# Delta rule in a small model's mixer: two units in step, value blocks inside the first inverse, an earlier gate slab, head norms by tokens, decay products on one engine

## What is computed

```python
def wkv7_scan(r, w, k, v, kk, a):
    def step(state, inp):
        r_t, w_t, k_t, v_t, kk_t, a_t = inp
        sk = jnp.einsum('bhvk,bhk->bhv', state, kk_t)
        state = (state * w_t[:, :, None, :]
                 - sk[..., None] * (a_t * kk_t)[:, :, None, :]
                 + v_t[..., None] * k_t[:, :, None, :])
        return state, jnp.einsum('bhvk,bhk->bhv', state, r_t)

# in rwkv7_time_mix (8 heads of 64):
    kk = heads(k * k_k)
    kk = kk / jnp.maximum(jnp.sqrt(jnp.sum(kk * kk, axis=-1, keepdims=True)), 1e-12)
    y = wkv7_scan(r_h, w_h, k_h, v_h, kk, a_h)
    mean = jnp.mean(y, axis=-1, keepdims=True)
    var = jnp.mean(jnp.square(y - mean), axis=-1, keepdims=True)
    y = (y - mean) * lax.rsqrt(var + EPS_GN)
    y = y * lnx_g + lnx_b
    y = (y + bonus) * g
```

## Time and profile before

| | us |
|---|---|
| median of 3 runs | 3098.65 (3093.9 to 3120.61) |
| profiled execution | 3099.2 |
| its span | 3097.6 |
| PE busy | 2847.0 (92%) |
| DVE busy | 1756.4 (57%) |
| ACT busy | 997.8 (32%) |
| POOL busy | 194.6 (6%) |

### The profile page before, as it was taken

One profiled execution on the slowest core, in us unless ns is written; L12 is line 12 of the kernel. 1 busy time (PEld: TensorE's weight loads), 2 busy tenths in 40 slices (PEclk: granted clock), 3 DMA queues, 4 the chain that ended last, 5 costly groups with the idle time before them and its releaser, 6 DMA issues.

```text
span 3097.6 us, 44761 instructions
## 1 busy us (share of the span) xinstructions
PE 2847.0 (92%) x18701; PEld 2328.5 (75%) x18701; DVE 1756.4 (57%) x2310; ACT 997.8 (32%) x1335; POOL 194.6 (6%) x244
## 2 busy tenths in 40 slices
PE   6979999988999999988889989999978899899997
PEld 6768888777678888767768768887657768688886
DVE  6667777768558777575364443334583473443334
ACT  5543222233442222242333332223432332332222
POOL 3100000000000000010040000000010040000000
PEclk9989999979999999899999999999888999999999
DMA  4214655412025555221003322222220012223221
GB/s 155 82 56 139 183 166 166 139 46 78 1 86 176 170 166 166 69 66 45 3 15 100 109 82 95 95 95 77 68 76 3 3 48 89 95 89 100 97 92 58
DMA packets 239083, 282.12 MB, mean 91 GB/s; under 512 B 7492, under 2 KB 225928, under 8 KB 238920
## 3 DMA queue, kind: packets, MB, share of 16 engines
q1 hardware_dynamic: 225598, 227.48, 23.1%
q0 software_dynamic: 12960, 52.14, 5.7%
q10 hardware_dynamic: 362, 0.11, 0.0%
HBM read 277.58 MB, written 2.10 MB: 90 GB/s over the span
## 4 chain that ended last, share of the span: by engine, by line
PE 80%; DVE 12%; ACT 4%; issue 3%; POOL 1%; DVEq 0%; ACTq 0%; POOLq 0%
PE psum L1853 22%; PE psum L1855 22%; PE psum L1854 22%; DVE wlo L1215 2%; PE psum L2197 1%; PE psum L1915 1%; ACT whi L730 1%; DVE mo L1613 1%; PE psum L2185 1%; ACT mo L1077 1%; PE psum L2114 1%; DVE rest L1229 1%; DVE rest L1742 1%; DVE rest L1234 1%; PE psum L2217 1%
## 5 line engine op out<-in xcount | busy, mean ns | idle before, releaser
L1853 PE MATMUL psum<-hh,whi 128*128 128x512 f32 x2112 | 841.1, 398 | 74.2 <-DVE wlo L1215 48.9
L1854 PE MATMUL psum<-hl,whi 128*128 128x512 f32 x2112 | 833.1, 394 | 0.0
L1855 PE MATMUL psum<-hh,wlo 128*128 128x512 f32 x2112 | 832.3, 394 | 0.0
L1215 DVE TENSOR_TENSOR wlo<-raw,whi 128x2048 fp32r<-128x2048 f32 x224 | 524.4, 2341 | 507.8 <-ACT whi L730 507.5
L730 ACT ACTIVATE whi<-raw 128x2048 fp32r<-128x2048 f32 x224 | 427.6, 1909 | 584.5 <-PE psum L1855 559.3
L1853 PEld LDWEIGHTS psum<-hh,whi 128*128 128x128 f32 x2112 | 403.8, 191 | 174.2 <-DVE wlo L1215 55.2
L1853 PE MATMUL psum<-mh,whi 128*128 128x512 f32 (+1 forms) x1184 | 459.5, 388 | 20.1 <-DVE ml L1387 9.0
L1854 PEld LDWEIGHTS psum<-hl,whi 128*128 128x128 f32 x2112 | 403.8, 191 | 84.8 <-issue 1.7
L1855 PEld LDWEIGHTS psum<-hh,wlo 128*128 128x128 f32 x2112 | 403.1, 191 | 85.2
L1854 PE MATMUL psum<-ml,whi 128*128 128x512 f32 (+1 forms) x1184 | 457.4, 386 | 0.0
L1855 PE MATMUL psum<-mh,wlo 128*128 128x512 f32 (+1 forms) x1184 | 457.3, 386 | 0.0
(11 more groups left out here) (350 smaller groups left out, 2847.8 us busy)
## 6 DMA issues: line engine op xcount, KB each, us to landing
rest<-in_ada_w POOLq DMA_DIRECT2D x64, 768.0 KB, 5.3
raw<-in_w_gu SPq DMA_DIRECT2D x44, 1024.0 KB, 5.0
raw<-in_w_in SPq DMA_DIRECT2D x34, 1024.0 KB, 5.3
raw<-in_w_mlp_in SPq DMA_DIRECT2D x32, 1024.0 KB, 5.7
raw<-in_w_mlp_out SPq DMA_DIRECT2D x32, 1024.0 KB, 5.3
raw<-in_w_out SPq DMA_DIRECT2D x16, 1024.0 KB, 5.1
raw<-in_w_down SPq DMA_DIRECT2D x16, 1024.0 KB, 5.1
raw<-in_w_mem_kv SPq DMA_DIRECT2D x8, 1024.0 KB, 5.3
```

What stands on the lines that cost most here:

```text
L1215: dve.tensor_tensor(wlo[:, g % 2, :, :], raw[:, g % 2, :, :], f32(whi[:, g % 2, :, :]), ALU.subtract)\
L1853: pe.matmul(out, whi_, xhi, start=first, stop=False)
L1854: pe.matmul(out, whi_, xlo, start=False, stop=False)
L1855: return pe.matmul(out, wlo_, xhi, start=False, stop=last)
```

## The change

1. **Two units in step.** `FILL` goes. Unit m's five levels alternate, in PE's, DVE's and ACT's programs and in `Plan`, with the solve, state steps and outputs of unit m - 1. The inverse `MM` and the token-major values `VT` get two buffers. WU, NU, WT and the second VT lie in the ring slot that the last z slab left (`ring_scratch`); SP therefore loads g1 only when the last output product is made. The last chunk's state isn't computed any more, since nothing reads it.
2. **Value blocks in the first inverse.** The second v2 slab's two blocks stand in unit 0's levels 0 and 1, the bonus sums in its level 4; key scaling, value mix and one decay product follow on DVE between the levels.
3. **Gate slab sooner.** z moves back by one unit; g0's parts are made at the end of unit 2, and g0's matmuls come behind the means, ahead of the variances.
4. **Norms by tokens.** `head_sums` puts 32 head sums in columns (16 matmuls of 2 columns), root and reciprocal run over 128x32, `head_factors` spreads them again (32 matmuls of 64 weight columns). It replaces the block sums for the key norm and for the variance; DVE multiplies straight from PSUM.
5. **Decay products.** KK, A2 and K2 by their decays are all DVE's now; R2's stays there. POOL keeps none.

The core of the diff (buffers, SP, POOL, DVE's start, PE's sums, unit loop and end):

```diff
-        WU, WT = carve(mo, 0, 8, P), carve(mo, 3 * Q, 4, P)
-        GS = carve(mo, 3 * Q + T, 2, 4, HD)
-        NU, HS = carve(mo, 6 * Q, 8, HD), carve(mo, 6 * Q + T, 2, 4, HD)
+        HS = carve(mo, 7 * Q + T, 2, 4, HD)
+
+
+        def ring_scratch(l):
+
+            r = raw[:, 1 - plan.slab["g0", (l, 0), 0] % 2, :, :].rearrange("p k n -> p (k n)")
+            wu = carve(r, 0, 8, P)
+            return wu, wu[:, :, 0:HD], carve(r, Q, 4, P), [VU, carve(r, Q + T, T)]
         mixed = [K2[:, t, :] for t in range(4)] + [A2[:, t, :] for t in range(4)]
...
                 for p in range(4):
                     for i, name in enumerate(("g0", "g1")):
+                        if (p, name) == (0, "g1"):
+                            ready(sp, J["Y", l, NT - 1, 1])
...
-                pool.tensor_tensor(KK, KK, SG, ALU.mult).then_inc(S("features"), 1)
-                pool.tensor_tensor(A2, A2, C2, ALU.mult).then_inc(S("features"), 1)
-                pool.wait_ge(S("features"), 4 * l + 4)
+                pool.wait_ge(S("rows_decayed"), 2 * l + 1)
                 pool.memset(MB, 0.0).then_inc(S("mb_zero"), 1)
...
@@ -1604,58 +1672,57 @@
                 dve.tensor_tensor(SG, C2, SG, ALU.subtract).then_inc(S("cum_decay"), 1)
 
                 dve.wait_ge(S("kk_raw"), 4 * l + 4)
-                for s in range(2):
-                    before_tiles(0, "r2", s, R2)
-                    for t in (2 * s, 2 * s + 1):
-                        evacuated(dve, J["kn", l, t])
-                        q.mark(dve.tensor_scalar(X1[:, t, :], X1[:, t, :], 1e-12, None, ALU.max))
-                        q.settle()
-                        q.mark(dve.reciprocal(X1[:, t, :], X1[:, t, :]))
-                        q.settle()
-                        q.mark(dve.tensor_tensor(KK[:, t, :], KK[:, t, :], X1[:, t, :], ALU.mult))
+                before_tiles(0, "r2", 0, R2)
+                evacuated(dve, J["kn", l])
+                q.mark(dve.tensor_scalar(hn[:, 0, :], hn[:, 0, :], 1e-12, None, ALU.max))
                 q.settle()
-                dve.sem_inc(S("kk_done"), 1)
+                dve.reciprocal(hn[:, 1, :], hn[:, 0, :]).then_inc(S("kk_inv"), 1)
+                lo(plan.slab["r2", l, 1] + 1)
+                before_part("r2", 1, 0, V("mu_shift_2", m0 + 2), R2[:, 2, :])
+                for t in range(4):
+                    j = J["kr", l, t]
+                    ready(dve, j)
+                    free(dve.tensor_tensor(KK[:, t, :], KK[:, t, :], bank(j), ALU.mult), j)
+                for t in range(4):
+                    evacuated(dve, J["kr", l, t])
 
                 evacuated(dve, J["la", l, 3])
                 dve.tensor_tensor(A2, X2, KK, ALU.mult).then_inc(S("b_made"), 1)
                 dve.wait_ge(S("b_made"), l + 1)
-                for t in range(4):
-                    q.mark(dve.tensor_scalar(X2[:, t, :], X2[:, t, :], 1.0, V("k_a_2", 4 * l + t), ALU.subtract, ALU.mult))
-                q.settle()
-                q.mark(dve.scalar_tensor_tensor(K2, X2, 1.0, K2, ALU.add, ALU.mult))
+                dve.wait_ge(S("decays"), 3 * l + 3)
+                dve.tensor_tensor(A2, A2, C2, ALU.mult).then_inc(S("keys_decayed"), 1)
+                dve.tensor_tensor(KK, KK, SG, ALU.mult).then_inc(S("keys_decayed"), 1)
+                before_part("r2", 1, 1, V("mu_shift_2", m0 + 3), R2[:, 3, :])
+                lo(plan.slab["v2", l, 1])
                 v_dst = VD if l else V2
-                before_tiles(2, "v2", 0, v_dst)
-                q.settle()
-
-                evacuated(dve, J["r2", l, 1, 1])
-                for t in range(4):
-                    dve.scalar_tensor_tensor(X2[:, t, :], R2[:, t, :], V("r_k_2", 4 * l + t), K2[:, t, :], ALU.mult, ALU.mult)\
-                       .then_inc(S("bonus_in"), 1)
-
-                dve.wait_ge(S("decays"), 3 * l + 3)
-                dve.wait_ge(S("bonus_in"), 4 * l + 4)
-                dve.tensor_tensor(K2, K2, C2, ALU.mult).then_inc(S("features"), 1)
                 q.mark(dve.tensor_copy(PC[:, :, :], X1[:, :, CH - 1:T:CH]))
                 q.mark(dve.memset(ST[:, 0, :, :], 0.0))
...
                 linear("k2", l, 1, h)
+                half = [slice(0, HD), slice(HD, P)]
+
+                def head_sums(p, ones, src):
+
+                    for b in range(NT):
+                        for t in range(4):
+                            ins = pe.matmul(p[:, 8 * b + 2 * t:8 * b + 2 * t + 2], src[:, t, b * P:(b + 1) * P], ones[:, 0:P:HD],
+                                            start=True, stop=True)
+                    return ins
+
+                def head_factors(p, t):
+
+                    for b in range(NT):
+                        for i in range(2):
+                            f = hn[:, 1, 8 * b + 2 * t + i:8 * b + 2 * t + i + 1].to_broadcast([P, HD])
+                            ins = pe.matmul(p[half[i], b * P:(b + 1) * P], f, ident[:, :], start=True, stop=True)
+                    return ins
+
...
                 pe.wait_ge(S("kk_sq"), l + 1)
+                done(head_sums(start("kn", l), sum_64, X1))
+                linear("r2", l, 1, h, only=0)
+                pe.wait_ge(S("kk_inv"), l + 1)
                 for t in range(4):
-                    p = start("kn", l, t)
-                    done(pe.matmul(p, sum_64[:, :], X1[:, t, :], start=True, stop=True))
-                linear("r2", l, 1, h)
-                for s in range(2):
-                    linear("v2", l, s, h)
-                for t in range(4):
-                    pe.wait_ge(S("bonus_in"), 4 * l + t + 1)
-                    p = start("bon", l, t)
-                    done(pe.matmul(p, sum_64[:, :], X2[:, t, :], start=True, stop=True))
-                pe.wait_ge(S("features"), 4 * l + 4)
+                    done(head_factors(start("kr", l, t), t))
+                linear("r2", l, 1, h, only=1)
+                linear("v2", l, 0, h)
+                pe.wait_ge(S("keys_decayed"), 2 * l + 2)
                 half = [slice(0, HD), slice(HD, P)]
                 chunk = [slice(0, CH), slice(CH, P)]
...
                                 if (t, c) == (3, 1):
                                     done(ins)
 
+                squares_of("L", 0, KK, A2)
+                squares_of("LT", 0, A2, KK)
+                for m in range(NT):
+                    level_left(m, 0)
+                    if m == 0:
+                        linear("v2", l, 1, h, only=0)
+                    if m:
+                        solve(m - 1)
+                    level_right(m, 0)
+                    if m:
+                        solve_turned(m - 1)
+                    level_left(m, 1)
+                    if m == 0:
+                        linear("v2", l, 1, h, only=1)
+                    if m:
+                        state_inputs(m - 1)
+                    level_right(m, 1)
+                    if m:
+                        state_step(m - 1, 0)
+                    level_left(m, 2)
+                    if m == 1:
+                        pe.wait_ge(S("rows_decayed"), 2 * l + 2)
+                    if m:
+                        products("Ark", m - 1, K2, R2)
+                        products("Arb", m - 1, A2, R2)
+                    level_right(m, 2)
+                    if m:
+                        values_new(m - 1)
+                    level_left(m, 3)
+                    if m:
+                        state_step(m - 1, 1)
+                    level_right(m, 3)
+                    if m:
+                        outputs(m - 1)
+                    level_left(m, 4)
+                    if m == 0:
+                        for t in range(4):
+                            pe.wait_ge(S("bonus_in"), 4 * l + t + 1)
+                            p = start("bon", l, t)
+                            done(pe.matmul(p, sum_64[:, :], X2[:, t, :], start=True, stop=True))
+                        pe.wait_ge(S("rows_decayed"), 2 * l + 1)
+                    for x in range(3):
+                        tokens(m, x)
+                    level_right(m, 4)
+                    tokens(m, 3)
+                    squares_of("Akk", m, K2, KK)
+                    if m + 1 < NT:
+                        squares_of("L", m + 1, KK, A2)
+                        squares_of("LT", m + 1, A2, KK)
+                    keys_times_values(m)
+                    inverse_turned(m)
+                    if m:
+                        linear("z", l, (m - 1) // 2, h, only=(m - 1) % 2)
+                m = NT - 1
+                solve(m)
+                solve_turned(m)
+                products("Ark", m, K2, R2)
+                state_inputs(m)
+                products("Arb", m, A2, R2)
+                state_step(m, 0)
+                linear("z", l, m // 2, h, only=m % 2)
+                values_new(m)
+                outputs(m)
+
                 for i in range(2):
...
                     evacuated(pe, J["Y", l, NT - 1, i])
                 for t in range(4):
                     p = start("gmean", l, t)
```

(20 more changed lines are left out.)

630 lines of the change are left out of this document (368 added, 262 removed).

## The result

The changed kernel takes 3066.53 us (median of four runs, 3060.72 to 3070.86) where the kernel before takes 3096.48 on the same chip: a ratio of 0.9886, with a 95% interval of 0.9851 to 0.9920. So it is faster, by 1.1%, and by about half of the 64 us that I had forecast; 3066.5 lies outside my range of 3015 to 3060, and beyond the 3047 to 3055 of rival 1. The profiled execution has a span of 3065.2 us against 3097.6, 32.4 less. Outside the stage nothing moved: the span less both stretches is 2522.7 us before (3097.6 - 280.8 - 294.1) and 2522.5 after.

A forecast was written before the change was run, and what follows sets the result against it. PE, busy 2847 of 3097.6 us, was taken to bound the kernel. Gains of 31.7 and 40.5 us in the two layers, together 72.2, less 8 for the clock, took 3099.2 to 3035; range 3015 to 3060.

The forecast's parts named there:

- rival 1: Across the stage: new sums and unfilled levels drop the clock; 3047, or 3055 with second layer's first unit low; chance 0.15.
- A: From the end of r2's first slab to the first inverse: forecast 32.9 us, against 60.8 before.
- D: From the mean sums to the branch projection: forecast 44.6 us, against 46.1 before.
- Unit 2: Steady delta-rule unit, level 0 to level 0: forecast 37.5 us, against 42.7 before.
- Rival 2: Steady units keep their 6.3 us of waits through in-order queues; 24 us lost, 3059; chance 0.12.
- rival 3: The two interleaved units run at half clock from the first level; slower, 3161; chance 0.02.
- rival 4: In A and D: norms by tokens gain nothing; factor matmuls at 0.28 us add 14 us a layer; 3063; chance 0.05.
- a unit of 40 us or more: Sign of a wrong forecast: a delta-rule unit this long, where steady ones were expected about 37.5 us apart.
- unit 3: Last delta-rule unit: forecast 38.3 us, with 2.3 more for the gate slab's parts and 1.5 less than a steady unit.
- Against this I set 8 us of clock: Over both layers, against the 72.2 us gain: 5 for four stretches of 2-column sums, 3 for a wait and unfilled levels.
- nothing, or about 20 if all of it runs at half clock: Bounds on the clock loss over both layers, which the forecast put at 8 us: none, or about 20 us.
- B: First inverse with v2's second slab and bonus sums: forecast 38.5 us in the first layer, 43.0 in the second.

The follow-up runs named there:

- the run with the added wait: The changed kernel with two useless wide DVE sums ahead of level 0's mask in unit 2; 3061.47 us in one run.
- the first inverse's run: The changed kernel with ACT's first operand turn, K2's decay product and the second layer's value passes moved in the first inverse; 3050.64 us, 0.9826 of before.

## Why the prediction was wrong, and where it was right

**The sum of work and waits: right in direction, close in most terms.** A (32.9, measured 32.75: work 30.92 and a wait of 1.83, where I had 30.9 and 2.0) and D at full clock (44.6; 44.28 once its rows stood apart) came out. Unit 2 did too (37.5; 37.47 and 37.74), but with some luck: I had 35.3 us of work and 2.2 of waits, 1.8 of them behind the third level, and the trace has 36.1 of work and 1.4 of idle time in pieces of at most 0.7. The 12.0 us wait for the slab went, and so did g1's. The filled levels worked: PE idle in a steady unit fell from 6.3 to 1.4 us. "Outside this stage nothing should move by more than 2 us" held (0.2). Rival 2, each unit keeping its 6.3 us of waits, and rival 3 are refuted; rival 4 too, since 64 records of factors take 3.71 us at full clock. (Rival 4's price was wrong as well: 64 records at 0.28 instead of 0.06 us are 14 us in A and 14 in D, so 56 over both layers and 3091, not 3063.) Of my own signs of being wrong, a unit of 40 us or more came true: unit 3 in both layers, and unit 1 of the second (40.35).

**The step that failed: "Against this I set 8 us of clock", and its bound, "nothing, or about 20 if all of it runs at half clock".** By comparing PE's busy time of a stretch with the same work at full or nearly full clock in an experiment, low clock took 1.6 us in A (32.49 less the other layer's 30.92), 9.8 in B (38.63 and 41.14 against 35.0 twice, at 0.95 and 0.96), 7.5 in unit 3 (39.95 and 38.38 against 35.54 and 35.27), and 11.0 in D (48.95 and 50.56 against 44.28): 29.9 us. That is 22 of the missing 32, and more than my upper bound. Three things were missed in it:

- Behind the variance sums I priced the next dense matmuls at half rate, 2.5 us at even odds for each of the four stretches of sums. For the key norm's sums that is what was seen (1.6 us in one layer and nothing in the other). But behind the variance's stand the gates and factors, where the clock stayed low for 10 and 14 us (6 to 7 in the later profile of the same kernel), and not for the 3.3 us of the dense block. I had walked the order of PE there for its length, and didn't ask what it does to the clock. The cost was 4.7 and 6.3 us.
- For the first inverse I put the second layer's bare levels and the 2.0 us wait at 3 us together. It was 9.8. The kernel before had shown the first inverse at 0.50 in both layers, and I took the v2 blocks in levels 0 and 1 to have cured it. Behind them the clock was back until level 2; levels 2 and 3 stayed bare. "Steady units with 6.3 us of waits held 1.00" was weak evidence for bare levels, since those units have fillers between their levels (products of 128 columns, a z block).
- Unit 3's fall I hadn't named. The wait of 2.2 us for the gate slab's low part was in my sum as 2.3; that it would drop the clock behind it was not.

**The other 10 us are waits and small terms.** Unit 3 with its wait and the clock at 1.00 takes 40.3 to 41.1 us, not 38.3 (the run with the added wait has 40.65 and 40.30): 4.3 over both layers. Unit 1 is 2.7 longer, with two and three rows of "issue" idle time of 0.4 to 1.4 us that I had not foreseen. The tail is 2.2 longer. B is 1.8 longer over both layers, as the rest of two errors: its work was 35.0 us in each layer where I had counted 32.0, and its waits were 5.2 and 8.2 us where I had put 6.5 and 11.0 (the 1.4 behind level 0 was 0.6). A and D give back 1.

**The rivals.** Rival 1 was the true case, in mechanism: "the new sums and the unfilled levels drop the clock each time and the small products that follow keep it low". Its price of 20 us was too low, and its chance of 0.15 too. The Trainium skill's rule that I had weighed there (TensorE: Matmul & The Clock Gate, Part 1: The HAM clock gate: half rate is the default, only activity releases it) is borne out by these traces in that D, with no PE wait at all, ran at 0.90 and 0.86, and it deserved a larger chance than I gave it.

**Part by part.** Two units in step, with their fillers, gave most: steady units 42.7 us apart became 37.5 to 40.4 at clock 1.00 (units 1 and 2), and the last unit's rest a drained tail of 20. Of A's 28 us, 14 are the v2 slab and bonus sums that stand in B now, 12 the wait; the key norm by tokens accounts for 5.7 to 7.2 us, by the run that put blocks back in another order. D's wait of 4.2 went to the gate slab and the variance by tokens together: with blocks behind the sooner gate slab 2.4 of it is left, so I put 1.8 down to the slab, as an estimate. D with the sooner slab and blocks takes 43.2, against 46.1 before. The variance by tokens lost 4 to 7 us a layer against that. The decay products on DVE gave about 1.5 a layer. The split between units in step and value blocks was read from stretches and not tried by itself.

## What to carry to other kernels

When an edit puts small matmuls in a row (sums of two columns, spreading, masks' products), price them and everything up to the next dense block at the half clock, and look for a dense block to put between two thin groups: the same matmuls in another order gave 3 and 6 us back here. Put fillers into every level of a dependent chain: a wait of 0.7 us mostly costs 0.7 among fillers, and more in a bare row. And ahead of a long in-order queue's critical operation, a 2.3 us operation that can wait should stand behind it; the wait it makes costs its length, and the clock on average half as much again.

## What the runs showed of the hardware that I had not expected

- The granted clock fell behind waits of no more than 0.7 us, in a row of 64x64 products (1430.01 in the first inverse's run), and in four of 18 stretches it did not fall behind a wait of 2.16 us (unit 3, in both layers of the run with the added wait among them, clock 1.00). The length of one wait is a poor guide.
- The same instructions with the same wait took 40.3 to 44.7 us in 18 stretches: the fall's place and extent change from profile to profile, and with edits elsewhere.
- Two-column sums lower the clock in some executions and places; a dense block behind them ran low for about 3.3 us and then recovered (0.63 to 0.40 us a matmul, seen once in the first layer's D), thin work for 6 to 14.
- A DVE copy of 128x32 elements took 4.54 and 4.56 us in the two layers, not 0.19, beside a wide POOL product, and ended with it. A short DVE operation is not safe beside POOL.
